# An indexer's products moved between projection products, its top-64 selection moved ahead, and a causal mask moved to another tile

## The chip, the cores and the metric

The kernel runs on one core of one Trainium2 chip. Its time is device time in microseconds (us) for one whole execution; the lower the better. The engines of a core work side by side, each through its own list of instructions: TensorE (PE in the profile; PEld is its weight load), VectorE (DVE), ScalarE (ACT), GpSimd (POOL) and SyncE (SP), which issues the DMA transfers. They wait for each other on counted semaphores.

## What is computed

The program is two transformer blocks on 256 tokens of width 1024, each with attention and a mixture of experts. The change lies in the mixer of the second block, after the first block's experts and before the recurrence of the second. All data is float32. One wide projection of the normed input gives, among others, queries (512 wide), a latent for keys and values (256), an indexer's query and key (8 heads of 32), and 15 groups of columns that are shifted by one token and mixed (called the shifted products here). The part that matters, for one block of 128 queries:

```python
dots = jnp.einsum('bthd,bsd->bths', qib, k_idx)
score = jnp.einsum('bths,bth->bts', jax.nn.relu(dots), wib) * idx_scale
score = jnp.where(causal[None], score, -jnp.inf)
_, sel = lax.top_k(score, top_k)          # top_k = 64 of 256
logits = jnp.einsum('bthd,btkhd->bthk', qb, k_sel) * (ATTN_HEAD_DIM ** -0.5)
logits = logits - slopes * dist           # dist = t - sel
logits = jnp.where(valid, logits, -jnp.inf)
p = jax.nn.softmax(logits, axis=-1)
# the shifted columns, for the recurrence that follows
mixed = p_shift + (prev - p_shift) * mu
# the modulation of the block
mod = jax.nn.silu(c) @ ada_w[i] + ada_b[i]
```

## The kernel before

Tokens lie in two halves (`t`) of 128. The code of a stage is split by engine: `project_*` and `sparse_*` follow each other in each engine's list, so their work overlaps. Order is by hand: each engine runs its list top to bottom and waits on semaphores.

**Projection and shifted products.** TensorE computes queries (`pj_q`), latent (`pj_kv`), indexer query (`pj_qi`), indexer key and head weights (`pj_ki`); ScalarE copies each out of PSUM (`pj_out`). A shifted product `m` of 0 to 14 (`shifted_product`, line 1806) accumulates 8 matmul pairs in the PSUM bank `SHIFT_BANKS[m]`. ScalarE evicts it with `shifted_own` (L1813), and VectorE adds the part of the previous token with `shifted_before` (L1820), which counts `mixed_done`. `SHIFT_NOW` of them come in `project_tensor`, those up to `LATE_SHIFT` = 11 in `sparse_tensor`, and the last four between head units. SyncE loads more gate weights when products 8, 12 and 15 are done.

**Modulation.** Rows of `ada_w_2` come in 8 chunks of 2 MB (`load_ada2`, L228) into two alternating slots of `side`. VectorE adds each with two instructions (`sum_ada2_rows`, L252, and `sum_ada2_cols`, L241); a chunk's load waits for the sums two chunks earlier.

**Indexer.** 16 dots (8 heads for each half, `dots`, L2077) each fill half a PSUM bank of banks 0 to 3; `relu` (L2185) evicts, `add_head` (L2237, L2239) weighs and sums into the tile `work`. It has four `rl` buffers. GpSimd masks each half (`affine_select`, L2061). VectorE then takes 8 rounds of `max` and `match_replace` (L2259, L2260) for each half, which leaves the 64 taken scores marked. `drop` turns the marks into 0 or -1, GpSimd masks it (L2065), and it is multiplied into the distance tile `dst2` (L2268).

**Attention.** The latent and the queries are transposed (L2087, L2092) and scaled by VectorE (`latT`, `qT2`); the up-projection makes keys and values (L2111); keys are normed (`head_norm`, L1839 to L1844, with a root on ScalarE) and transposed (L2119). Sixteen units (head and half) follow: `scores` (L2132), bias and mask by VectorE (`first`, L2276), `max`, exponential on ScalarE (L2209), a turn (L2142), the product with values (L2151).

**Later.** The recurrence, the merge of branches, and the second experts stage follow. SyncE issues the first expert load of that stage (`load_group`, L995) once VectorE has counted `or_done`.

Of the kernel before, what the change touches and what calls it, by code (L numbers as in the profile page):

```python
# [47 lines left out]
def build(nc, inp, out, debug=None, until=99):  # L48
    ctx = ExitStack()
    with ctx:  # L50
# [1699 lines left out]
        if debug and until <= 5:  # L1750
# [9 lines left out]
            "pj_out": ("pj_q_out", "pj_q_out", "pj_kv_out", "q_sq", "lat_sq", "lat_sq", "pj_qi_out", "pj_ki_out", "pj_ki_out", "lat_root", "q_root"),  # L1760
# [31 lines left out]
        SHIFT_NOW = 5  # L1792
        SHIFT_BANKS = [0, 1, 2, 3, 4, 7, 4, 7, 5, 6, 4, 7, 7, 7, 7]
# [28 lines left out]


# [37 lines left out]
        if True:  # L1861
# [55 lines left out]
            def project_tensor(pe):  # L1917
# [34 lines left out]
                for m in range(SHIFT_NOW):  # L1952
                    if m == 4:
                        pe.wait_ge(sem("pj_out"), at("pj_ki_out", 2))
                    shifted_product(pe, m)

            def project_scalar(act):
# [20 lines left out]
                act.wait_ge(sem("norm_vec"), at("lat_ms", 1))  # L1978
                act.activation(st6[:, 4:6], st6[:, 2:4], ACT.Sqrt).then_inc(sem("pj_out"), 1)
                act.wait_ge(sem("norm_vec"), at("q_ms", 1))  # L1980
                act.activation(st6[:, 32:48], st6[:, 16:32], ACT.Sqrt).then_inc(sem("pj_out"), 1)
# [37 lines left out]
        work = side[:, 4608:5120].rearrange("p (t s) -> p t s", t=NT)  # L2019
# [4 lines left out]
        rl = acc[:, 1024:2048].rearrange("p (b s) -> p b s", b=4)  # L2024
# [20 lines left out]
        if True:  # L2045
# [8 lines left out]
            def sparse_pool(pool):  # L2054
                pool.wait_ge(sem("ada2_rows_summed"), ADA2_CHUNKS)
                pool.wait_ge(sem("ada2_cols_summed"), ADA2_CHUNKS)
                pool.iota(dst2, pattern=[[P, NT], [-1, S]], base=0, channel_multiplier=1,
                          allow_small_or_imprecise_dtypes=True).then_inc(sem("dst2"), 1)
# [4 lines left out]
                pool.wait_ge(sem("drop_raw"), 1)  # L2063
                for t in range(NT):
                    pool.affine_select(out=drop[:, t, :], in_=drop[:, t, :], compare_op=ALU.is_ge, fill=-1.0, base=t * P,  # L2065
                                       pattern=[[-1, S]], channel_multiplier=1).then_inc(sem("drop"), 1)

            def sparse_tensor(pe):

                def dots(u):  # L2070
                    t, h = u // 8, u % 8
                    r = 32 * (h % 4)
                    if u >= 4:
                        pe.wait_ge(sem("idx_relu"), u - 3)
                    else:
                        pe.wait_ge(sem("mixed_done"), u + 1)
                    pe.matmul(ps[h % 4][:, 0:S], qiT[r:r + 32, h // 4, t * P:(t + 1) * P], kiT[r:r + 32, :],  # L2077
                              start=True, stop=True).then_inc(sem("idx_dots"), 1)
                for u in range(4):
                    dots(u)  # L2080
                shifted_product(pe, SHIFT_NOW)

                pe.wait_ge(sem("mixed_done"), SHIFT_NOW)
                pe.wait_ge(sem("norm_vec"), at("lat_normed", 1))
                for c in range(2):
                    for t in range(NT):
                        last = pe.transpose(ps[4][:, c * S + t * P:c * S + (t + 1) * P], kvl[:, t, c * P:(c + 1) * P], ident[:, :])  # L2087
# [978 lines left out]
```

## Time and profile before

| what | value |
|---|---|
| median of 3 runs | 1456.38 us (1456.31 to 1458.89) |
| the profiled execution | 1454.63 us |
| its span in the trace | 1452.9 us |
| mean granted TensorE clock (share of full) | 0.886 |
| TensorE busy | 1163.4 us, 80% |
| VectorE busy | 502.4 us, 35% |
| ScalarE busy | 265.6 us, 18% |
| GpSimd busy | 42.2 us, 3% |
| share of DMA in the chain that ended last | 25% |
| DMA moved | 404.66 MB, 279 GB/s mean |

All times inside the kernel are counted from the start of the span. A clock of 1.00 is 2.4 GHz and 0.50 is 1.2 GHz. In a timeline, a row merges instructions of one form that follow each other; the number in brackets is how long the engine stood idle before it, and who released it. A busy TensorE matmul row overlaps the next a little, because matmuls are pipelined.

### The profile page before, as it was taken

The numbers are of one execution on the slowest core, as the hardware profiler recorded it, in microseconds if no ns is written. First come the engines' busy times: TensorE is split into PE (matmuls) and PEld (weight loads), VectorE is DVE, ScalarE is ACT, GpSimd is POOL, SyncE is SP. The second block draws the span as 40 slices with busy tenths as digits, with TensorE's granted clock in tenths as the row PEclk, the third lists the DMA queues.
The fourth block names the chain that finished last, engine by engine and source line by source line (L and its number), as shares of the span: only waits on it lengthen the run. The fifth ranks groups of instructions, "written<-read, shape, count | busy, mean of one in ns | idle before, by whom it ended". The sixth has DMA issues, their size and how long they took to land. (4 is left out here: it accounts for less than half of the span.)

```text
span 1452.9 us, 16891 instructions
## 1 busy us (share of the span) xinstructions
PE 1163.4 (80%) x6663; PEld 677.1 (47%) x6663; DVE 502.4 (35%) x1285; ACT 265.6 (18%) x666; POOL 42.2 (3%) x109
## 2 busy tenths in 40 slices
PE   5999869999999693889999999979656567666666
PEld 2788444444343482566777776644121221221212
DVE  1569442222222526665644446342101011010111
ACT  2233212111121210234322220012010100101000
POOL 0000000000000200000101100000000000000000
PEclk8999879999999796898999997989877787778888
DMA  9877636999999748032001112555999999999995
GB/s 372 281 276 276 252 119 265 403 429 427 426 429 404 226 171 332 1 116 102 15 1 59 59 58 64 232 231 226 422 422 422 422 422 422 422 422 422 422 421 246
DMA packets 75149, 404.66 MB, mean 279 GB/s; under 512 B 14073, under 2 KB 15286, under 8 KB 41304
## 3 DMA queue, kind: packets, MB, share of 16 engines
q1 hardware_dynamic: 75096, 403.94, 68.9%
q8 instruction: 35, 0.57, 0.2%
q14 instruction: 18, 0.15, 0.0%
HBM read 402.88 MB, written 1.05 MB: 278 GB/s over the span
## 5 line engine op out<-in xcount | busy, mean ns | idle before, releaser
L1178 PE MATMUL ps<-ring,hT_sb 128*32 128x512 f32 x768 | 115.9, 759 | 72.8 <-DMA ring<-in_expert_w_gate 41.7
L1538 PE MATMUL ps<-ring,hT_sb 128*64 128x512 f32 x448 | 113.1, 594 | 3.5 <-ACT hT_sb L1609 1.8
L1178 PEld LDWEIGHTS ps<-ring,hT_sb 128*32 128x32 f32 x768 | 28.5, 135 | 154.5 <-issue 90.8
L1178 PE MATMUL ps<-side,hT_sb 128*32 128x512 f32 x256 | 42.9, 831 | 36.7 <-DMA side<-in_expert_w_up 18.9
L634 PE MATMUL ps<-hT_sb,ring 128*128 128x256 f32 x256 | 62.1, 393 | 2.7 <-ACT hT_sb L379 2.7
L1190 PE MATMUL ps<-ring,tmp 128*32 128x512 f32 x384 | 49.7, 664 | 18.2 <-DMA ring<-in_expert_w_down 18.2
L1244 ACT ACTIVATE hT_sb<-ps,modc 128x128 f32<-128x128 f32 x72 | 27.1, 457 | 191.3 <-PE ps L1161 191.3
L1806 PE MATMUL ps<-hT_sb,ring 128*128 128x256 f32 (+1 forms) x240 | 61.8, 419 | 0.0
L1538 PEld LDWEIGHTS ps<-ring,hT_sb 128*64 128x64 f32 x448 | 35.3, 137 | 55.0 <-issue 51.8
L1282 DVE TENSOR_TENSOR tmp<-ps,tmp 128x512 f32<-128x512 f32 x8 | 5.5, 692 | 151.8 <-ACT tmp L1252 151.8
L1546 PE MATMUL ps<-ring,tmp 128*64 128x512 f32 x256 | 56.7, 595 | 0.0
L634 PEld LDWEIGHTS ps<-hT_sb,ring 128*128 128x128 f32 x256 | 48.1, 195 | 13.7 <-issue 4.6
L1806 PEld LDWEIGHTS ps<-hT_sb,ring 128*128 128x128 f32 (+1 forms) x240 | 48.3, 205 | 10.7 <-issue 2.8
L1293 DVE COPY hT_sb<-ps 128x512 f32<-128x512 f32 x8 | 5.5, 692 | 134.8 <-PE ps L1190 134.8
L1609 ACT ACTIVATE hT_sb<-ps,modc 128x128 f32<-128x128 f32 x72 | 27.1, 457 | 127.0 <-PE ps L1528 127.0
L2628 PE MATMUL ps<-hT_sb,ring 128*128 128x128 f32 x384 | 49.2, 281 | 0.0
L2628 PEld LDWEIGHTS ps<-hT_sb,ring 128*128 128x128 f32 x384 | 44.7, 191 | 5.4 <-issue 4.5
L1178 PEld LDWEIGHTS ps<-side,hT_sb 128*32 128x32 f32 x256 | 9.8, 146 | 69.7 <-issue 26.5
L1190 PE MATMUL ps<-side,tmp 128*32 128x512 f32 x128 | 24.3, 931 | 19.8 <-DMA side<-in_expert_w_down 19.8
L1288 DVE TENSOR_TENSOR tmp<-ps,tmp 128x512 f32<-128x512 f32 x8 | 5.5, 692 | 92.2 <-PE ps L1178 92.2
L214 DVE SCALAR_TENSOR_TENSOR acc<-side,cond,acc 128x1024 f32<-128x1024 f32 x28 | 35.8, 1280 | 0.8
L1190 PEld LDWEIGHTS ps<-ring,tmp 128*32 128x32 f32 x384 | 12.1, 120 | 49.4 <-issue 26.7
(522 smaller groups left out, 1917.1 us busy)
## 6 DMA issues: line engine op xcount, KB each, us to landing
ring<-in_expert_w_gate SPq DMA_DIRECT2D x12, 4096.0 KB, 34.6
ring<-in_expert_w_up SPq DMA_DIRECT2D x12, 4096.0 KB, 34.7
ring<-in_expert_w_down SPq DMA_DIRECT2D x12, 4096.0 KB, 34.2
ring<-in_expert_w_down SPq DMA_DIRECT2D x16, 2048.0 KB, 15.5
ring<-in_expert_w_up SPq DMA_DIRECT2D x16, 2048.0 KB, 17.9
ring<-in_expert_w_gate SPq DMA_DIRECT2D x12, 2048.0 KB, 19.5
side<-in_ada_w SPq DMA_DIRECT2D x20, 1024.0 KB, 6.5
ring<-in_w_in SPq DMA_DIRECT2D x9, 2048.0 KB, 8.3
```

What stands on the lines that cost most here:

```text
L214: ins = v.scalar_tensor_tensor(a, w, s, a, ALU.mult, ALU.add)
L634: last = pe.matmul(ps[6][:, w * S:(w + 1) * S], cell(2 * w + h // 4)[:, c, (h % 4) * P:(h % 4 + 1) * P], hT[:, c, :], start=(c == 0), stop ...
L1178: last = pe.matmul(bank[es, :], xg[:, c, es], w[:, e, c % 4, :], start=(c == 0), stop=(c == KC - 1))
L1190: last = pe.matmul(out_ps[h][es, :], hidT[:, f, es], w[:, e, f % 2, h * 512:(h + 1) * 512], start=(f == 0), stop=(f == FC - 1))
L1244: last = act.activation(xg[:, c, :], (gate_ps, up_ps)[half][:, (c % 4) * P:(c % 4 + 1) * P], ACT.Identity, scale=modc[:, 2 * KC + c:2 * KC ...
L1282: v.tensor_tensor(hid, gate_ps[:, :], hid, ALU.mult).then_inc(sem("q_silu"), 1)
L1288: v.tensor_tensor(hid, up_ps[:, :], hid, ALU.mult).then_inc(sem("q_hid_done"), 1)
L1538: last = pe.matmul(bank[e * SLOTS:(e + 1) * SLOTS, :], xg[:, c, e * SLOTS:(e + 1) * SLOTS], dst(e, j, par)[:, c, :], start=(c == 0), stop= ...
L1546: last = pe.matmul(out_ps[h][e * SLOTS:(e + 1) * SLOTS, :], hidT[:, f, e * SLOTS:(e + 1) * SLOTS], dst(e, 2, 0)[:, f, h * 512:(h + 1) * 51 ...
L1609: last = act.activation(xg[:, c, :], (gate_ps, up_ps)[half][:, (c % 4) * P:(c % 4 + 1) * P], ACT.Identity, scale=modc[:, 2 * KC + c:2 * KC ...
L1806: last = pe.matmul(ps[SHIFT_BANKS[m]][0:n, 0:S], p2(i)[:, c, o:o + n], hT[:, c, :], start=(c == 0), stop=(c == KC - 1))
L2628: last = pe.matmul(gate_bank(i), p2(GATE0 + m // 4)[:, c, (m % 4) * P:(m % 4 + 1) * P], hT[:, c, t * P:(t + 1) * P], start=(c == 0), stop= ...
```

## The change

- In `project_tensor`, four dots stand ahead of each of the shifted products 0 to 3, and all 16 are done there; products 4 and 5 follow (`SHIFT_NOW` = 6). The wait for ScalarE's copies of indexer key and head weights comes ahead of all of them. Banks 0 to 3 are the dots' and banks 4 to 7 the shifted products'.
- ScalarE takes the two roots (latent and query norm) ahead of the indexer's copies; relus of four dots precede each `shifted_own`. `rl` has eight buffers.
- VectorE sums four chunks of the modulation, not two, ahead of the latent and query norms. After each of the chunks 4 to 7 it adds four heads and evicts one shifted product.
- Top-64 starts right behind. Turns of the latent, the queries and the keys, the key norm and the evictions 4 to 8 are put between its rounds (`BESIDE`); evictions 9 and 10 come behind the distance step.
- GpSimd makes the distance tile, masks both halves of the scores, and then writes 1.0e32 into the non-causal places of the distance tile. The two selects on `drop` are gone. `work` moves from `side` to `acc`.
- In `sparse_tensor` the order is: transposes of latent and queries, product 6, up-projection, product 7, key transposes, products 8 and 9, the first four scores, product 10. The square of the keys stands behind the second of ScalarE's four copies.

```diff
-            "pj_out": ("pj_q_out", "pj_q_out", "pj_kv_out", "q_sq", "lat_sq", "lat_sq", "pj_qi_out", "pj_ki_out", "pj_ki_out", "lat_root", "q_root"),
+            "pj_out": ("pj_q_out", "pj_q_out", "pj_kv_out", "q_sq", "lat_sq", "lat_sq", "lat_root", "q_root", "pj_qi_out", "pj_ki_out", "pj_ki_out"),
...
-        SHIFT_NOW = 5
-        SHIFT_BANKS = [0, 1, 2, 3, 4, 7, 4, 7, 5, 6, 4, 7, 7, 7, 7]
+        SHIFT_NOW = 6
+        SHIFT_BANKS = [4, 5, 6, 7, 4, 5, 6, 7, 4, 5, 6, 7, 7, 7, 7]
...
+        def dots(pe, u):
+            t, h = u // 8, u % 8
+            r = 32 * (h % 4)
+            if u >= 4:
+                pe.wait_ge(sem("idx_relu"), u - 3)
+            pe.matmul(ps[h % 4][:, 0:S], qiT[r:r + 32, h // 4, t * P:(t + 1) * P], kiT[r:r + 32, :],
+                      start=True, stop=True).then_inc(sem("idx_dots"), 1)
+
+        def relu(act, u):
+            act.wait_ge(sem("idx_dots"), u + 1)
+            if u >= RL:
+                act.wait_ge(sem("idx_added"), u - RL + 1)
+            act.activation(rl[:, u % RL, :], ps[u % 4][:, 0:S], ACT.Relu).then_inc(sem("idx_relu"), 1)
+
+        def add_head(v, u):
+            t, h = u // 8, u % 8
+            v.wait_ge(sem("idx_relu"), u + 1)
+            w = w_idx[:, t * 8 + h:t * 8 + h + 1]
+            if h == 0:
+                ins = v.tensor_scalar(work[:, t, :], rl[:, u % RL, :], w, None, ALU.mult)
+            else:
+                ins = v.scalar_tensor_tensor(work[:, t, :], rl[:, u % RL, :], w, work[:, t, :], ALU.mult, ALU.add)
+            ins.then_inc(sem("idx_added"), 1)
+            v.wait_ge(sem("idx_added"), u + 1)
+            if h == 7:
+                v.tensor_copy(st6[:, 200 + t:201 + t], work[:, t, 0:1]).then_inc(sem("idx_score"), 1)
...
-                for m in range(SHIFT_NOW):
-                    if m == 4:
-                        pe.wait_ge(sem("pj_out"), at("pj_ki_out", 2))
+                pe.wait_ge(sem("pj_out"), at("pj_ki_out", 2))
+                for m in range(4):
+                    for u in range(4 * m, 4 * m + 4):
+                        dots(pe, u)
+                    shifted_product(pe, m)
+                for m in range(4, SHIFT_NOW):
                     shifted_product(pe, m)
...
+                act.wait_ge(sem("norm_vec"), at("lat_ms", 1))
+                act.activation(st6[:, 4:6], st6[:, 2:4], ACT.Sqrt).then_inc(sem("pj_out"), 1)
+                act.wait_ge(sem("norm_vec"), at("q_ms", 1))
+                act.activation(st6[:, 32:48], st6[:, 16:32], ACT.Sqrt).then_inc(sem("pj_out"), 1)
...
-                for m in range(SHIFT_NOW):
+                for m in range(4):
+                    for u in range(4 * m, 4 * m + 4):
+                        relu(act, u)
+                    shifted_own(act, m)
+                for m in range(4, SHIFT_NOW):
                     shifted_own(act, m)
...
-                for k in range(2):
+                for k in range(4):
...
-                for k in range(2, ADA2_CHUNKS):
-                    if k >= 5:
-                        shifted_before(v, k - 5)
+                for k in range(4, ADA2_CHUNKS):
                     sum_ada2_rows(v, k)
                     sum_ada2_cols(v, k)
-                for m in range(3, SHIFT_NOW):
-                    shifted_before(v, m)
+                    for u in range(4 * (k - 4), 4 * (k - 4) + 4):
+                        add_head(v, u)
+                    shifted_before(v, k - 4)
...
-        work = side[:, 4608:5120].rearrange("p (t s) -> p t s", t=NT)
+        work = acc[:, 5120:5632].rearrange("p (t s) -> p t s", t=NT)
...
-                pool.iota(dst2, pattern=[[P, NT], [-1, S]], base=0, channel_multiplier=1,
-                          allow_small_or_imprecise_dtypes=True).then_inc(sem("dst2"), 1)
+                p_step(pool.iota(dst2, pattern=[[P, NT], [-1, S]], base=0, channel_multiplier=1,
+                                 allow_small_or_imprecise_dtypes=True))
                 for t in range(NT):
                     pool.wait_ge(sem("idx_score"), t + 1)
                     pool.affine_select(out=work[:, t, :], in_=work[:, t, :], compare_op=ALU.is_ge, fill=-BIG, base=t * P,
                                        pattern=[[-1, S]], channel_multiplier=1).then_inc(sem("idx_causal"), 1)
-                pool.wait_ge(sem("drop_raw"), 1)
                 for t in range(NT):
-                    pool.affine_select(out=drop[:, t, :], in_=drop[:, t, :], compare_op=ALU.is_ge, fill=-1.0, base=t * P,
-                                       pattern=[[-1, S]], channel_multiplier=1).then_inc(sem("drop"), 1)
+                    ins = pool.affine_select(out=dst2[:, t, :], in_=dst2[:, t, :], compare_op=ALU.is_ge, fill=1.0e32, base=t * P,
+                                             pattern=[[-1, S]], channel_multiplier=1)
+                ins.then_inc(sem("dst2"), 1)
...
+                pe.wait_ge(sem("idx_relu"), 16)
                 pe.wait_ge(sem("norm_vec"), at("lat_normed", 1))
...
+                shifted_product(pe, SHIFT_NOW)
...
+                shifted_product(pe, SHIFT_NOW + 1)
                 pe.wait_ge(sem("norm_vec"), at("k_normed", 1))
+                pe.wait_ge(sem("turn_out"), at("qT_done", 4))
...
-                for u in range(4):
-                    scores(u)
-
-                pe.wait_ge(sem("kv_out"), 4)
-                for m in range(SHIFT_NOW + 1, LATE_SHIFT):
+                for m in range(SHIFT_NOW + 2, LATE_SHIFT):
+                    if m == LATE_SHIFT - 1:
+                        for u in range(4):
+                            scores(u)
                     shifted_product(pe, m)
                 pe.wait_ge(sem("mixed_done"), LATE_SHIFT)
...
+                    if i == 1:
+                        act.wait_ge(sem("kv_out"), 2)
+                        act.activation(sq6, side[:, 0:1024], ACT.Square).then_inc(sem("k_act"), 1)
...
+                BESIDE = {1: (4,), 3: (5,), 4: (turn_lat, turn_q), 5: (6,), 6: ("k", 7), 7: (turn_k, 8)}
...
-                    if r in (3, 4, 6, 7):
-                        shifted_before(v, {3: 6, 4: 7, 6: 8, 7: 9}[r])
-                shifted_before(v, 10)
-                v.tensor_scalar(drop, work, TAKEN, 1.0, ALU.is_equal, ALU.subtract).then_inc(sem("drop_raw"), 1)
+                    for x in BESIDE.get(r, ()):
+                        if x == "k":
+                            head_norm(v, sq6, 48, "k_act", "k", side[:, 0:1024])
+                        elif isinstance(x, int):
+                            shifted_before(v, x)
+                        else:
+                            x()
+                v_step(v.tensor_scalar(drop, work, TAKEN, 1.0, ALU.is_equal, ALU.subtract))
                 v.wait_ge(sem("dst2"), 1)
-                v.wait_ge(sem("drop"), 2)
-
                 v_step(v.scalar_tensor_tensor(dst2, drop, -1.0e32, dst2, ALU.mult, ALU.add))
+                for m in range(9, LATE_SHIFT):
+                    shifted_before(v, m)
```

## Rows read from the trace of the kernel before

**Rows 1.** The chain that ended last, in order of time (start us, us, what).

```profile
979.63 0.07 issue
...
1010.37 29.20 DMA side<-in_expert_w_gate
```

**Rows 2.** Timeline of SyncE's queue (start us, us, engine, line, operation), 680 to 1010.

```profile
909.91 17.57 SPq L995 DMA_DIRECT2D ring<-in_expert_w_gate  x2
```

**Rows 3.** Stretches: length, each engine's busy us (instructions), TensorE's granted clock, DMA share, GB/s.

```profile
520.00:525.00 5.00, 5.00 (x25) 4.41 (x24) 0.17 (x1) 2.33 (x6) 0.00 (x0) 1.00 0.68 251
535.00:540.00 5.00, 5.00 (x17) 4.10 (x16) 4.63 (x6) 0.65 (x2) 0.00 (x0) 0.66 0.00 2
585.00:600.00 15.00, 11.73 (x53) 6.25 (x51) 9.52 (x21) 7.53 (x19) 0.40 (x1) 1.00 0.00 1
631.00:638.00 7.00, 6.53 (x22) 4.87 (x23) 3.81 (x14) 2.71 (x10) 0.00 (x0) 0.52 0.01 2
674.00:910.00 236.00, 218.22 (x1764) 179.12 (x1762) 127.87 (x365) 62.48 (x177) 22.31 (x53) 0.94 0.14 48
```

**Rows 4.** Timeline of VectorE, 510 to 690 (idle before it and its releaser in brackets).

```profile
534.82 0.17 DVE L2002 RECIPROCAL acc<-acc 128x2 f32<-128x2 f32 x1 [11.88 <-ACT acc L1979]
...
550.85 2.35 DVE L252 SCALAR_TENSOR_TENSOR gate_rows<-side,cond,gate_rows 128x2048 f32<-128x2048 f32 x1 [2.96 <-DMA side<-in_ada_w]
...
561.16 2.35 DVE L252 SCALAR_TENSOR_TENSOR gate_rows<-side,cond,gate_rows 128x2048 f32<-128x2048 f32 x1 [5.30 <-DMA side<-in_ada_w]
...
578.20 0.87 DVE L1820 SCALAR_TENSOR_TENSOR ring<-ps,colsB,ring 128x255 f32<-128x255 f32 x2
...
588.92 3.61 DVE L2239 SCALAR_TENSOR_TENSOR side<-acc,small,side 128x256 f32<-128x256 f32 x7
...
596.78 1.22 DVE L1839 TENSOR_REDUCE acc<-acc 128x16 f32<-128x1024 f32 x1 [4.05 <-ACT acc L2197]
...
605.59 0.41 DVE L2259 MAX8 acc<-side 128x8 f32<-128x256 f32 x1
...
607.54 0.43 DVE L2259 MAX8 acc<-side 128x8 f32<-128x256 f32 x1
...
629.68 0.42 DVE L2276 SCALAR_TENSOR_TENSOR acc<-side,ps 128x256 f32<-128x256 f32 x1
```

**Rows 5.** Timeline of SyncE's queue, 500 to 680.

```profile
543.39 0.33 SPq L228 DMA_DIRECT2D side<-in_ada_w  x1
...
547.92 18.21 SPq L228 DMA_DIRECT2D side<-in_ada_w  x3
```

**Rows 6.** Timeline of TensorE, 500 to 680.

```profile
530.57 3.63 PE L1945 MATMUL ps<-tmp,hT_sb 128*128 128x8 f32 x32
534.06 19.20 PE L1806 MATMUL ps<-hT_sb,ring 128*128 128x256 f32 x80
...
579.88 5.30 PE L1806 MATMUL ps<-hT_sb,ring 128*128 128x256 f32 x16
...
585.45 1.04 PE L2092 MATMUL ps<-ident,tmp 128*128 128x128 f32 x8
586.42 1.11 PE L2077 MATMUL ps<-tmp 32*128 32x256 f32 x8
587.46 3.70 PE L2111 MATMUL ps<-ring,side 128*128 128x512 f32 x8
...
607.73 18.85 PE L1806 MATMUL ps<-hT_sb,ring 128*128 128x256 f32 x80
...
643.03 0.70 PE L2132 MATMUL ps<-side 64*128 64x256 f32 x4
```

**Rows 7.** Timeline of ScalarE, 500 to 680.

```profile
527.32 0.60 ACT L1973 ACTIVATE tmp<-ps 128x512 f32<-128x512 f32 x1 [4.57 <-PE ps L1937]
...
627.11 1.28 ACT L2209 ACT_TABLE_LOAD   x1
```

**Rows 8.** Timeline of GpSimd, 500 to 680.

```profile
604.25 0.40 POOL L2061 TENSOR_SCALAR_AFFINE_SELECT side<-side 128x256 f32<-128x256 f32 x1 [10.97 <-DVE acc L2243]
```

More of the change, by code:

```diff
@@ L2086, in sparse_tensor @@
                     for t in range(NT):
-                        last = pe.transpose(ps[4][:, c * S + t * P:c * S + (t + 1) * P], kvl[:, t, c * P:(c + 1) * P], ident[:, :])
+                        last = pe.transpose(ps[2][:, c * S + t * P:c * S + (t + 1) * P], kvl[:, t, c * P:(c + 1) * P], ident[:, :])
                 last.then_inc(sem("turn_psum"), 1)
@@ L2091, in sparse_tensor @@
                     for t in range(NT):
-                        last = pe.transpose(ps[5 + c // 2][:, (c % 2) * S + t * P:(c % 2) * S + (t + 1) * P],
+                        last = pe.transpose(ps[c // 2][:, (c % 2) * S + t * P:(c % 2) * S + (t + 1) * P],
                                             q_tok[:, t, c * P:(c + 1) * P], ident[:, :])
                 last.then_inc(sem("turn_psum"), 1)
-                for u in range(4, 8):
-                    dots(u)
+                shifted_product(pe, SHIFT_NOW)
                 pe.wait_ge(sem("kv_up_loaded"), 16)
-                pe.wait_ge(sem("mixed_done"), SHIFT_NOW + 1)
                 pe.wait_ge(sem("turn_out"), at("latT_done", 2))
@@ L2102, in sparse_tensor @@
                     for t in range(NT):
-                        if n == 0 and t == 1:
-                            pe.wait_ge(sem("turn_out"), at("latT_done", 2))
                         if n == 1:
                             pe.wait_ge(sem("kv_out"), t + 1)
-                            if t == 0:
-                                pe.wait_ge(sem("turn_out"), at("qT_done", 4))
-                        b = ps[7] if (t == 0) else ps[4]
                         for c in range(2):
-                            last = pe.matmul(b[:, :], latT[:, c, t * P:(t + 1) * P], kv_up[:, c, n * 512:(n + 1) * 512],
+                            last = pe.matmul(ps[3 - t][:, :], latT[:, c, t * P:(t + 1) * P], kv_up[:, c, n * 512:(n + 1) * 512],
                                              start=(c == 0), stop=(c == 1))
                         last.then_inc(sem("kv_psum"), 1)
-                for u in range(8, 16):
-                    dots(u)
+                shifted_product(pe, SHIFT_NOW + 1)
                 pe.wait_ge(sem("norm_vec"), at("k_normed", 1))
+                pe.wait_ge(sem("turn_out"), at("qT_done", 4))
                 for c in range(4):
                     for t in range(NT):
-                        last = pe.transpose(ps[5 + c // 2][:, (c % 2) * S + t * P:(c % 2) * S + (t + 1) * P],
+                        last = pe.transpose(ps[c // 2][:, (c % 2) * S + t * P:(c % 2) * S + (t + 1) * P],
                                             k_tok[:, t, c * P:(c + 1) * P], ident[:, :])
@@ L2179, in sparse_scalar @@
             def sparse_scalar(act):
-                def relu(u):
-                    act.wait_ge(sem("idx_dots"), u + 1)
-                    if u >= 4:
-                        act.wait_ge(sem("idx_added"), u - 3)
-                    act.activation(rl[:, u % 4, :], ps[u % 4][:, 0:S], ACT.Relu).then_inc(sem("idx_relu"), 1)
                 shifted_own(act, SHIFT_NOW)
-                for u in range(8):
-                    relu(u)
                 act.wait_ge(sem("ada2_rows_summed"), ADA2_CHUNKS)
@@ L2244, in sparse_vector, with turn_lat @@
-                for u in range(8):
-                    add_head(u)
-                head_norm(v, sq6, 48, "k_act", "k", side[:, 0:1024])
-                for u in range(8, 16):
-                    add_head(u)
-                v.wait_ge(sem("turn_psum"), at("k_psum", 1))
-                for c in range(4):
-                    v.tensor_scalar(kT2[:, c, :], ps[5 + c // 2][:, (c % 2) * S:(c % 2 + 1) * S], colsB[:, nB + 1:nB + 2], None,
-                                    ALU.mult).then_inc(sem("turn_out"), 1)
+                def turn_lat():
+                    v.wait_ge(sem("turn_psum"), at("lat_psum", 1))
+                    for c in range(2):
+                        v.tensor_scalar(latT[:, c, :], ps[2][:, c * S:(c + 1) * S], colB("kv_norm_g_2", c), None, ALU.mult).then_inc(
+                            sem("turn_out"), 1)
@@ new lines, in turn_q, with turn_k @@
+                def turn_q():
+                    v.wait_ge(sem("turn_psum"), at("q_psum", 1))
+                    for c in range(4):
+                        v.tensor_scalar(qT2[:, c, :], ps[c // 2][:, (c % 2) * S:(c % 2 + 1) * S], qk_cols[:, 1:2], None,
+                                        ALU.mult).then_inc(sem("turn_out"), 1)
+                def turn_k():
+                    v.wait_ge(sem("turn_psum"), at("k_psum", 1))
+                    for c in range(4):
+                        v.tensor_scalar(kT2[:, c, :], ps[c // 2][:, (c % 2) * S:(c % 2 + 1) * S], colsB[:, nB + 1:nB + 2], None,
+                                        ALU.mult).then_inc(sem("turn_out"), 1)
```

50 lines of the change are left out of this document (4 added, 46 removed).

## The prediction

> **What bounds the kernel now.** I read the page first: its chain of work that ended last is mostly transfers of expert weights. Followed in order of time, the chain begins only at 979.6 us, and from 1010 us on nearly every long piece of it is such a transfer [rows 1]. So the end is a stream of fixed length. What can be won is an earlier start of it, and the chain says nothing of the stage that the change edits. The SyncE queue says when the stream starts: its first expert load goes out at 909.91, behind a wait on the branch results (`or_done`) that VectorE makes [rows 2]. Between 674 and 910 TensorE is 92% busy and the DMA moves 48 GB/s [rows 3]: that stretch is compute, ordered by waits among engines, and each load in it is issued on a signal of an engine, not at a fixed time. A shift of the attention stage should therefore reach the end one for one.
>
> In the attention stage I read the VectorE timeline, then TensorE's. VectorE waits until 534.82 for a root that ScalarE runs behind its copies, then waits for three of the modulation's weight chunks (2.96 us for chunk 4, 5.30 for chunk 5), since a chunk's load needs the sum two chunks back [rows 4, 5]. TensorE finishes its five shifted products at about 553.3 and then does next to nothing till 579.9: each indexer product waits for an evicted bank, and the evictions stand between the sums [rows 6]. Only at 605.59 does top-64 start. The first biased logits come at 629.68 [rows 4]. That instruction is my mark: what it gains, the kernel gains.
>
> **The change, laid out in time.** I place the new order on the trace's clock; until about 500 us nothing differs.
>
> *Loads and sums.* Now four chunks are summed before the latent norm. The DMA has delivered all that was issued by about 523 (it moved 251 GB/s from 520 to 525 and its next load is issued at 543.39), chunk 3 ahead of the last weights [rows 3, 5]. One chunk costs VectorE two instructions of 2.35 us, 2.27 from start to start, so 4.54 us [rows 4]. Sums 2 and 3 fit from about 513 to 522.5, where VectorE idled, and cost nothing; if they had no such gap they would cost 9.1 us. Chunk 4 can then be asked for at about 517 instead of 543.39 and chunk 5 at 522.6 instead of 547.9 [rows 5]. SyncE is freed earlier for the weights queued behind them, p2_load(4) and p2_load(5). The two roots moved ahead of the indexer's copies should end at about 526; ScalarE idled 4.57 us before the first of those copies at 527.32, so they delay none [rows 7].
>
> *Dots, products, evictions.* TensorE now waits for both copies and starts at 534.8 instead of 534.06, +0.7 us (the root behind these copies released VectorE at 534.82) [rows 4, 6]. Four dots take 1.11 us at the full clock [rows 6]; one shifted product takes 3.45 (five take 18.85 with a slow start, and 3.45 is what separates their evictions). The first five took 19.20, so product 0 took about 5.4: the granted clock was 0.66 of full from 535 to 540 though TensorE was busy [rows 3, 6]. I keep that loss of 1.9 us, part of it (0.3) now on dots: dots end 536.1, product 0 at 540.9, its two evictions at 542.05 (0.2 + 0.47 ScalarE, then 0.40 VectorE). Chunk 4's sum ends near 532.5 and heads 0 to 3 are added before 539, so VectorE waits for this eviction before sum 5, and everything later in the stretch hangs on it.
>
> From 542.05, three rounds of sum (4.54), four head sums (4 x 0.516 = 2.06, from seven in 3.61) and one eviction (0.40; two take 0.87, overlapping a little) are 7.0 us each [rows 4]. Chunk 6 was asked for at 532.6. Chunk 7 is asked for at 546.6 and needed at 556.1, 9.5 us later; the load issued at 543.39 took 7.5 us till its sum began [rows 4, 5]. The last head sum ends at 542.05 + 21.0 - 0.4 = 562.65. GpSimd masks in 0.40, plus 0.3 for two hand-overs [rows 8]: top-64 starts at 563.35, against 605.59. TensorE has four groups of 4.56, two products and the transposes of latent and queries (about 1.4) and product 6; it is done at 566.2. Its waits on relu have slack: relu 15 needs head 7 added, which is so at 548.7.
>
> *Work moved into the rounds.* A round of top-64 for both halves is 1.95 us [rows 4]. Five rounds and evictions 4 and 5 (0.8) end at 573.9, and the two turns of the latent, each as large as an eviction (0.87 for both), bring 574.75. Here lies the new stall: the latent up-projection, queued on TensorE ahead of product 7, waits for it from 566.2, and with it ScalarE's key copies and the key norm. From there TensorE sets the mark: up-projection 2 x 3.45 (its 3.70 overlaps the next), product 7 3.45, key transposes 1.0 (the query's eight took 1.04), products 8 and 9 6.9, four scores 1.35 (two take 0.70), product 10 3.45 [rows 6]. That is 23.05. To it comes the clock: after waits like this one TensorE ran at 1.2 GHz, and the product at 579.88 took 5.30, a loss of 1.85 [rows 6]. Lower bound 0 (the clock holds), upper 3.5 (6.9 us at half the clock do the work of 3.45); I take 2.4, between this 1.85 and the loss of about 3 behind the first unit's wait, where the clock stood at 0.52 from 631 to 638 [rows 3]. 574.75 + 23.05 + 2.4 = 600.2. Two evictions (0.2 + 0.47 + 0.40): VectorE's first biased logits at 601.3.
>
> *VectorE beside it.* Rounds 5 to 7, the key norm (3.1 us, 596.78 to the next head sum), the key's and query's turns and evictions 6 to 9 amount to some 15 us in the 26.5 between 574.75 and 601.3, so they are hidden, although the wait for product 7 holds round 7 back to about 588.5. If VectorE had no slack there, the worst is the key norm plus a turn, 4.7 us. The mask in the distance tile takes GpSimd's two selects out of the path. Before, they and the drop and distance steps stood between the last eviction and the logits (the eviction that needs product 10, whose five end at 626.6, and the mark at 629.68 [rows 4, 6]: 3.1 us). Now drop and distance run at about 593 to 594, under product 9, and 1.1 us remain between product 10 and the mark. These 2 us are in the difference of the marks already. The exponential's table load (1.28, at 627.11 right behind the last eviction by ScalarE) now runs from 600.9 to 602.15; the first maximum is ready at 602.3, 1.0 behind the mark, so the load stays hidden by 0.15 us; at worst it costs 0.3 [rows 7].
>
> **Sum.** Mark 629.68 - 601.3 = 28.4 us. The 16 head units behind the mark keep their order and banks. Profiled execution 1454.63 (span 1452.9) gives 1426.2. The median shown is 1456.38, 1.75 above it, so I predict 1456.4 - 28.4 = **1428.0 us**.
>
> **Rivals.**
> 1. *The chunks stay late (0.10).* Chunk 5 took 13.2 us before, sharing the DMA with other weights [rows 4, 5]. If chunk 7 takes that too it lands at 559.9, not 556.1: +3.7, 1431.7. For it: weights p2(5) follow in the queue. Against it: they follow chunk 7 in the queue and do not precede it.
> 2. *More low clock or a stall among the rounds (0.07).* Product 0 wholly slow (+1.5) and the key norm uncovered (+4.7) give about 1434. ScalarE and TensorE slack above speaks against it.
> 3. *The clock stays up (0.07).* The wait before the up-projection costs nothing (-2.4) and the wait behind product 10, 2.9 instead of 4.9 us, no longer slows the 6 us of work behind it (-3.1) [rows 3, 6]: 1422.5.
> 4. *The gain is given back at a later wait (0.02).* A load of the recurrence or of the experts would have to be bound to an absolute time: 1456.4. The queue shows none.
> 5. *Slower (0.03): interleaved narrow dots hold TensorE at 1.2 GHz.* All of its 53 us of work from 534.8 to 600.2 then take twice as long: 4 x 9.1, then 13.8, 2.8, 6.9 put the up-projection at 594.7 and product 10 at 640.7, the mark at 641.8: +12.1, 1468.5. It decides once some 41 of the 53 us run at the low clock (28.4 of gain, 8.6 of TensorE's own wait, and the 4.3 that I assume already). For it: the clock was low at 535 to 540 right after the 8-column products. Against it: from 585 to 600 dots, transposes and copies alternated and the clock was 1.00 [rows 3, 6]. The Trainium skill, page "TensorE: Matmul & The Clock Gate", section "A second HAM failure mode: psum-queue depth-cycling", says that small idle gaps between groups of matmuls that cycle through PSUM banks can make the clock swing between its two levels. By that page rival 5 would gain weight; this trace's 585 to 600 does not show it.
>
> **How the numbers follow.** The forecast holds 0.71, with its own range 1424.5 to 1431.5. Rivals 1 to 3 lie inside 1422 to 1436, which is my range; outside it are rivals 4 and 5 and a tail. "No change" means within 0.2%, 2.9 us, about what a measurement of this kernel can tell from nothing. Faster 0.95, same 0.02, slower 0.03.
>
> **What the profile after will show.** Top-64 starts near 563, the up-projection near 575 after a wait of some 8 us, the first biased logits near 601; the first expert load is issued near 881.5. Dots come in four groups with products between and no waits on evictions. The clock is 1.00 between about 541 and 569. I am wrong if chunk sums wait for DMA after 550, if TensorE is at half clock across the dots, or if the first expert load moves by less than the mark.

## The result and the profile after

The changed kernel takes 1419.34 us (median of 4 runs, 1417.30 to 1421.82) against 1456.35 us (4 runs, 1455.33 to 1458.89): ratio 0.9744, 95% interval 0.9723 to 0.9765, so 37 us less. I had forecast 28.4 us less and a range that ended at 1422. The direction was right, and the sum fell short by 8.7 us. The profiled execution took 1417.3 us, 37.3 less than the one of before.

The page of the changed kernel, its span and the granted clock in 40 slices:

```profile
span 1415.6 us, 16890 instructions
...
PEclk8999878999999799899999997979778787888888
```

SyncE's queue and the chain that ended last, of the changed kernel (start us, us, what):

```profile
873.23 17.25 SPq L995 DMA_DIRECT2D ring<-in_expert_w_gate  x2
```

```profile
942.64 0.07 issue
```

The first expert load goes out 36.7 us earlier than in [rows 2], and the chain begins 37.0 earlier than in [rows 1]. From that load to the end of the span it is 543.0 us before and 542.4 after, so nearly all that was won was won before it. (Over all 14 profiles of this document this last part took 542.2 to 545.2 us; it is fixed only to some 3 us.) VectorE's timeline of the changed kernel, in answer to [rows 4]:

```profile
519.81 2.35 DVE L252 SCALAR_TENSOR_TENSOR gate_rows<-side,cond,gate_rows 128x2048 f32<-128x2048 f32 x1 [0.29 <-DMA side<-in_ada_w]
...
530.07 2.35 DVE L252 SCALAR_TENSOR_TENSOR gate_rows<-side,cond,gate_rows 128x2048 f32<-128x2048 f32 x1 [1.27 <-DMA side<-in_ada_w]
...
541.63 0.48 DVE L1820 SCALAR_TENSOR_TENSOR ring<-ps,colsB,ring 128x255 f32<-128x255 f32 x1 [3.49 <-ACT ring L1813]
...
555.96 2.34 DVE L252 SCALAR_TENSOR_TENSOR gate_rows<-side,cond,gate_rows 128x2048 f32<-128x2048 f32 x1
...
563.28 0.43 DVE L2250 MAX8 acc<-acc 128x8 f32<-128x256 f32 x1
...
573.89 0.88 DVE L2229 TENSOR_SCALAR side<-ps,colsB 128x256 f32<-128x256 f32 x2
...
596.35 0.48 DVE L1820 SCALAR_TENSOR_TENSOR ring<-ps,colsB,ring 128x255 f32<-128x255 f32 x1 [1.98 <-ACT ring L1813]
601.00 0.48 DVE L1820 SCALAR_TENSOR_TENSOR ring<-ps,colsB,ring 128x255 f32<-128x255 f32 x1 [4.16 <-ACT ring L1813]
601.39 0.41 DVE L2271 SCALAR_TENSOR_TENSOR acc<-side,ps 128x256 f32<-128x256 f32 x1
```

And TensorE's, in answer to [rows 6]:

```profile
535.01 0.77 PE L1829 MATMUL ps<-tmp 32*128 32x256 f32 x8 [0.64 <-ACT small L2011]
535.71 5.30 PE L1806 MATMUL ps<-hT_sb,ring 128*128 128x256 f32 x16
...
561.95 3.62 PE L1806 MATMUL ps<-hT_sb,ring 128*128 128x256 f32 x16
574.92 9.58 PE L2125 MATMUL ps<-ring,side 128*128 128x512 f32 x16 [9.35 <-DVE side L2229]
...
596.73 3.72 PE L1806 MATMUL ps<-hT_sb,ring 128*128 128x256 f32 x16
603.18 0.41 PE L2156 MATMUL ps<-ident,acc 128*128 128x128 f32 x2 [2.73 <-issue]
```

The reader is to see two things. Up to the mark (the first biased logits, L2276 before and L2271 after) the layout holds almost to the tenth: top-64 at 563.28 (forecast 563.35), the start of the up-projection at 574.92 (574.75), 9.42 us from there to the start of product 7 (9.3), the mark at 601.39 (601.3). The wait ahead of the up-projection was 9.35 us, where the forecast gives 8.55. The mark came 28.3 us earlier. Behind it, where the code is the same in both, another 8.4 us went: from the mark to the first expert load it is 280.2 us before and 271.8 after.

Where they went shows in a table of stretches, cut at the same distances behind the mark (10.3, 20, 11, 12 us). Columns as in [rows 3]; the number ahead of the DMA share is the granted clock. The kernel before:

```profile
629.70:640.00 10.30, 8.53 (x33) 6.71 (x34) 6.27 (x22) 3.33 (x11) 0.19 (x2) 0.67 0.01 2
640.00:660.00 20.00, 18.44 (x113) 13.79 (x112) 12.20 (x47) 10.03 (x33) 0.00 (x0) 1.00 0.31 105
660.00:671.00 11.00, 8.86 (x44) 5.25 (x43) 4.28 (x17) 2.77 (x9) 0.00 (x0) 0.84 0.16 40
671.00:683.00 12.00, 12.00 (x39) 9.43 (x39) 9.52 (x18) 5.31 (x11) 0.00 (x0) 0.57 0.36 139
```

The changed kernel:

```profile
601.40:611.70 10.30, 8.52 (x42) 6.50 (x42) 6.40 (x23) 5.08 (x15) 0.00 (x0) 0.83 0.01 2
611.70:631.70 20.00, 17.66 (x109) 13.44 (x107) 13.31 (x51) 9.53 (x32) 0.00 (x0) 1.00 0.31 106
631.70:642.70 11.00, 9.64 (x57) 6.84 (x58) 4.95 (x19) 4.67 (x12) 0.00 (x0) 1.00 0.44 148
642.70:654.70 12.00, 12.00 (x78) 10.20 (x77) 11.79 (x14) 10.35 (x18) 0.00 (x0) 1.00 0.57 195
```

The units and the preparation of the recurrence run at 1.2 GHz for about 6.8, 3.5 and 10.3 us before (twice the missing clock share times the length: (1 - 0.67) x 10.3 x 2, and so on), and for 3.5 us in all after. That difference of 17 us at half the clock is worth at most 8.5 us, and the two timelines drift apart by 1.4 us at the second unit, by 3.0 at the last, and by 7.4 at the reciprocal of the preparation (687.78 before, 652.11 after). The last 1.0 us goes with one more low stretch, which runs up to the first expert load in both kernels. It begins 19.6 us ahead of that load before and 16.8 us ahead of it after (an estimate from the clock shares of the last 20 us, before first):

```profile
889.91:909.91 20.00, 19.32 (x176) 13.16 (x176) 12.14 (x26) 2.85 (x7) 1.12 (x5) 0.51 0.25 76
853.23:873.23 20.00, 18.39 (x176) 12.25 (x176) 12.53 (x27) 2.85 (x7) 1.12 (x5) 0.58 0.27 83
```

The question for the experiments was what made the clock differ.

### The profile page after: what moved, and what is told of

Same layout as the page of the kernel before. It is cut to its first block and busy times, and to the rows that moved or that the text cites. A ratio compares the mean times of both kernels' runs of the same rounds, so it can differ in the third digit from the quotient of the medians.

```text
span 1415.6 us, 16890 instructions
## 1 busy us (share of the span) xinstructions
PE 1145.7 (81%) x6663; PEld 665.5 (47%) x6663; DVE 502.5 (35%) x1285; ACT 265.5 (19%) x666; POOL 42.1 (3%) x109
## 5 line engine op out<-in xcount | busy, mean ns | idle before, releaser
L1178 PEld LDWEIGHTS ps<-ring,hT_sb 128*32 128x32 f32 x768 | 28.4, 134 | 154.8 <-issue 90.7
L1806 PE MATMUL ps<-hT_sb,ring 128*128 128x256 f32 (+1 forms) x240 | 57.7, 394 | 0.0
L634 PEld LDWEIGHTS ps<-hT_sb,ring 128*128 128x128 f32 x256 | 48.2, 195 | 13.8 <-issue 4.6
L1806 PEld LDWEIGHTS ps<-hT_sb,ring 128*128 128x128 f32 (+1 forms) x240 | 44.9, 192 | 9.3 <-issue 2.2
L2623 PE MATMUL ps<-hT_sb,ring 128*128 128x128 f32 x384 | 49.2, 281 | 0.0
```

Of the source, the lines that this page charges most:

```text
L634: last = pe.matmul(ps[6][:, w * S:(w + 1) * S], cell(2 * w + h // 4)[:, c, (h % 4) * P:(h % 4 + 1) * P], hT[:, c, :], start=(c == 0), stop ...
L1178: last = pe.matmul(bank[es, :], xg[:, c, es], w[:, e, c % 4, :], start=(c == 0), stop=(c == KC - 1))
L1806: last = pe.matmul(ps[SHIFT_BANKS[m]][0:n, 0:S], p2(i)[:, c, o:o + n], hT[:, c, :], start=(c == 0), stop=(c == KC - 1))
L2623: last = pe.matmul(gate_bank(i), p2(GATE0 + m // 4)[:, c, (m % 4) * P:(m % 4 + 1) * P], hT[:, c, t * P:(t + 1) * P], start=(c == 0), stop= ...
```

## The experiments

Two theories. The first: the instants at which the clock can fall or rise are not tied to the work, so which waits cost something is decided by where they happen to lie, and a small shift moves the end by something other than itself. The rival: the new order keeps TensorE's waits short (2.73 us instead of 4.9 ahead of the first unit), so the 8.4 us belong to the change. Profiles of different runs of one order place top-64 up to 2.5 us apart, so I compare the mark with an earlier instruction of the same trace, or give the time behind the mark ("tail": from the mark to the first expert load). The groups of runs were measured on different chips, each with the kernel before beside it (medians 1454.31 to 1457.03), so ends of different groups are compared by their ratios.

**Delays.** VectorE fills a tile that is not in use, ahead of the turn of the latent (changed kernel) or of the keys (before). One fill took 0.91 us, and from one to the next it is 1.19.

```diff
                 def turn_lat():
+                    for _ in range(2):        # or 4
+                        v_step(v.memset(side[:, 6144:7168], 0.0))
```

> The changed kernel, with two dummy fills of an unused 128x1024 tile (about 0.6 us each) on VectorE ahead of the latent's turn: everything behind it starts about 1.3 us later, nothing else differs. Where the instants at which TensorE's clock falls and rises are not tied to the work (first theory), the first biased logits come 1.3 us later but the end moves by something else, between 0 and +9 us, because other waits of the head units and of the preparation now meet a fall. Where the new order of the work is what keeps the clock up (rival), the end moves by 1.3 us and the clock falls once between 601 and 670, as in the changed kernel.

> As the run with two fills, with four: 2.6 us later. First theory: the end moves by something between 0 and +10 us, and not twice what two fills gave. Rival: +2.6 us.

> The kernel before, with two such fills on VectorE ahead of the turn of the keys, which TensorE's first scores and VectorE's top-64 both wait for: everything behind starts about 1.3 us later. First theory: the end moves by anything between +1.3 and -7 us, since the three low stretches behind the first biased logits (6.8, 3.4 and 10.2 us) need not recur. Rival: +1.3 us, with the three low stretches.

> As the run before, with four fills: 2.6 us later. The first biased logits then stand to the clock's instants about as in the changed kernel, so the first theory expects the low stretches behind them to shrink from 20 us towards 3 and the end to come earlier although work was added: some -5 us. Rival: +2.6 us.

Measured, with the profile's numbers beside the medians:

| kernel | median us | ratio to before (95%) | mark | tail |
|---|---|---|---|---|
| before | 1456.35 | | 629.68 | 280.2 |
| changed | 1419.34 | 0.9744 (0.9723 to 0.9765) | 601.39 | 271.8 |
| after_late2 | 1422.74 | 0.9784 (0.9750 to 0.9819) | 603.63 | 272.1 |
| after_late4 | 1433.68 | 0.9839 (0.9821 to 0.9857) | 607.34 | 281.0 |
| before_late2 | 1460.36 | 1.0020 (1.0009 to 1.0031) | 634.02 | 280.4 |
| before_late4 | 1454.30 | 0.9984 (0.9974 to 0.9994) | 634.55 | 274.5 |

Four fills cost the changed kernel 14.3 us (13.8 by the ratios), although they keep VectorE busy for only 3.6: counted from top-64 the mark comes 4.1 us later (607.34 - 565.15 against 601.39 - 563.28), and the tail is 9.1 us longer. Two fills cost 3.4 and left the tail alone. On the kernel before, two fills cost 3.3 us and left the tail alone too, while four made the end come earlier (1454.30 against 1457.03 for the kernel before beside it, interval below 1): 3.6 us of useless VectorE work more, 2.7 us less time. The stretches of the changed kernel with four fills, cut like those above:

```profile
607.30:617.60 10.30, 8.48 (x32) 6.57 (x33) 6.07 (x22) 4.23 (x12) 0.00 (x0) 0.67 0.01 2
...
637.60:648.60 11.00, 8.96 (x42) 5.10 (x42) 4.46 (x18) 2.72 (x9) 0.00 (x0) 0.84 0.12 30
648.60:660.60 12.00, 11.91 (x38) 9.33 (x39) 9.50 (x19) 5.47 (x11) 0.00 (x0) 0.57 0.39 148
```

They are the low stretches of the kernel before, clock for clock, in the order of the changed one. The rival, by which four fills move the end by about their own length and leave the tail alone, falls. So does its reason, the shorter wait ahead of the first unit: that wait is 2.73 us in the changed kernel and in after_late4 alike, with 3.4 us of low clock behind it in the one and 6.8 in the other. My sizes were loose: a fill took 0.91 us, not 0.6, and before_late4 shrank its low stretches from 20 to 10 us, not to 3.

**One part alone, and one part undone.** The mask on the kernel before, and the old mask on the changed kernel:

```diff
-                pool.wait_ge(sem("drop_raw"), 1)
                 for t in range(NT):
-                    pool.affine_select(out=drop[:, t, :], in_=drop[:, t, :], compare_op=ALU.is_ge, fill=-1.0, base=t * P,
-                                       pattern=[[-1, S]], channel_multiplier=1).then_inc(sem("drop"), 1)
+                    ins = pool.affine_select(out=dst2[:, t, :], in_=dst2[:, t, :], compare_op=ALU.is_ge, fill=1.0e32, base=t * P,
+                                             pattern=[[-1, S]], channel_multiplier=1)
...
-                v.wait_ge(sem("drop"), 2)
```

> The kernel before with one part of the change alone: GpSimd writes the causal mask into the distance tile ahead of time instead of into the drop tile in the path. It takes out VectorE's wait for GpSimd (1.01 us before), so the first biased logits come 1.0 us earlier. If a shift were carried through one for one, the end would come 1.0 us earlier; by the theory of the clock's instants it moves by that plus something between -7 and +4 us from the low stretches behind.

> The changed kernel with the old mask (GpSimd's two selects on the drop tile in the path). In the new order drop and distance run under product 9, where VectorE then waits 1.98 us for ScalarE's eviction, so the wait for GpSimd (about 1.0) is hidden: first biased logits unmoved, end within 0.5 us of the changed kernel. Rival: the mask carries part of the gain here too, and the mark comes 1 us later.

before_mask: 1446.15 us, ratio 0.9937 (0.9916 to 0.9957). From top-64 to the mark it took 23.2 us instead of 24.1, so the mark gained 0.9, as expected. The end gained about 9, more than I had allowed, since the tail fell from 280.2 to 271.9. TensorE's wait ahead of the first unit is 3.92 us instead of 4.89, and only 3.4 us of low clock followed:

```profile
631.64 0.41 PE L2142 MATMUL ps<-ident,acc 128*128 128x128 f32 x2 [3.92 <-issue]
...
634.26 2.59 PE L1806 MATMUL ps<-hT_sb,ring 128*128 128x256 f32 x8
```

The half product that took 2.59 us here took 3.57 in the kernel before and 1.95 at the full clock.

after_old_mask: 1419.44 us, ratio 0.9751 (0.9733 to 0.9769), 0.1 us from the changed kernel; top-64 to mark 38.1 us in both. Its VectorE timeline shows the cover that I had named:

```profile
596.22 0.69 DVE L2263 SCALAR_TENSOR_TENSOR side<-side 128x512 f32<-128x512 f32 x1 [1.01 <-POOL side L2099]
597.91 0.48 DVE L1820 SCALAR_TENSOR_TENSOR ring<-ps,colsB,ring 128x255 f32<-128x255 f32 x1 [0.99 <-ACT ring L1813]
```

The wait for GpSimd is back (1.01), and the wait for the eviction behind it is shorter by as much (0.99 instead of 1.98). In the new order the mask carries nothing.

**The chunks.**

```diff
-                for k in range(4):            # ahead of the latent norm
+                for k in range(2):
...
+                for k in (2, 3):              # behind the query norm
+                    sum_ada2_rows(v, k)
+                    sum_ada2_cols(v, k)
```

> The changed kernel, but only two chunks of the modulation are summed ahead of the latent and query norms; chunks 2 and 3 come behind them. Their 9.1 us are no longer in VectorE's gap, and the loads of chunks 4 to 7 are asked for 8 to 13 us later, so VectorE waits for the DMA again. I expect top-64 to start at about 571 instead of 563.3 and the first biased logits 8 us later. If this part carried nothing, both would stay.

1435.18 us, ratio 0.9862 (0.9843 to 0.9881): 15.8 us slower than the changed kernel (17 by the ratios). Top-64 starts at 572.3, 9.0 us later where I had put 8, and the mark is at 609.4, 8.0 us later, as expected; the waits for the DMA are back:

```profile
539.65 2.35 DVE L252 SCALAR_TENSOR_TENSOR gate_rows<-side,cond,gate_rows 128x2048 f32<-128x2048 f32 x1 [2.92 <-DMA side<-in_ada_w]
551.06 2.35 DVE L252 SCALAR_TENSOR_TENSOR gate_rows<-side,cond,gate_rows 128x2048 f32<-128x2048 f32 x1 [4.45 <-DMA side<-in_ada_w]
```

The tail is the long one, 280.3 us, so the rest is again clock.

**TensorE kept at work.** The direct test of what the low clock costs: matmuls whose result nobody reads, in the wait ahead of the first unit (10 on the kernel before, 5 on the changed one, with and without the four fills).

```diff
+                pe.wait_ge(sem("mixed_done"), 8)
+                for _ in range(10):
+                    pe.matmul(ps[7][:, S:2 * S], ident[:, :], hT[:, 0, :], start=True, stop=True)
                 pe.wait_ge(sem("mixed_done"), LATE_SHIFT)
```

> The kernel before with ten matmuls whose result nobody reads (128x256, about 0.43 us each at the full clock), placed on TensorE in its 4.9 us wait ahead of the first head unit. They move nothing ahead of the first biased logits. If the low clock behind that wait is what makes the stretch from the mark to the first expert load 280.2 us long instead of 271.8, the first low stretch (6.8 us from 630.9) goes and the end comes 2 to 8 us earlier, although work was added. If the low clock costs nothing because other engines set the pace of the units, the end stays within 1 us.

> The changed kernel with five such matmuls in its 2.7 us wait ahead of the first unit. There only 3.4 us of low clock are behind the mark, so at most 1.7 us are to be had: end 0 to 2 us earlier than the changed kernel.

> The changed kernel delayed by four dummy fills (3.6 us of VectorE time ahead of the latent's turn, which alone cost 14.3 us at the end, 8 to 9 of them behind the mark), and with the five matmuls ahead of the first unit. If the wait ahead of the first unit is where the loss behind the mark begins, the filler brings the tail back from 281.0 to about 272 and the end to about 1424. If the loss comes from where the later waits happen to lie, the tail stays at 278 or more and the end near 1432.

| kernel | median us | ratio to before (95%) | mark | tail |
|---|---|---|---|---|
| before_filled | 1447.18 | 0.9947 (0.9932 to 0.9962) | 631.31 | 270.7 |
| after_filled | 1417.38 | 0.9746 (0.9732 to 0.9760) | 601.90 | 271.8 |
| after_filled_late4 | 1425.13 | 0.9802 (0.9785 to 0.9820) | 606.85 | 272.5 |

Added work alone made the kernel before 7.1 us faster (1454.31 to 1447.18, measured side by side). The stretches of before_filled behind its mark:

```profile
631.30:641.60 10.30, 9.28 (x56) 7.04 (x54) 7.32 (x26) 5.43 (x18) 0.23 (x2) 1.00 0.12 30
...
661.60:672.60 11.00, 9.76 (x57) 6.94 (x56) 5.22 (x17) 5.16 (x12) 0.00 (x0) 1.00 0.55 192
672.60:684.60 12.00, 12.00 (x86) 10.66 (x85) 11.83 (x11) 10.32 (x16) 0.00 (x0) 1.00 0.51 175
```

All three low stretches are gone, the later two as well, though nothing was put into the waits ahead of those. Its tail, 270.7 us, is 9.5 shorter than that of before and about that of the changed kernel, and nothing of the change is in it. On the changed kernel the filler brings nothing that can be told from zero (ratio 0.9746 against 0.9744), and the tail stays at 271.8. The low stretch behind the first unit's wait is gone there, but another of the same length appears 29.8 us behind the mark, where the changed kernel has none:

```profile
601.90:612.20 10.30, 9.28 (x56) 7.04 (x54) 7.33 (x27) 6.30 (x19) 0.00 (x0) 1.00 0.13 30
...
632.20:643.20 11.00, 9.76 (x51) 6.49 (x50) 3.66 (x14) 3.54 (x8) 0.00 (x0) 0.87 0.42 149
```

With four fills the filler takes 8.5 us off the tail (281.0 to 272.5), again with one low stretch of 3.4 us among the units, 28.9 us behind the mark. The end comes 8.6 us earlier by the medians and 5.4 by the ratios (0.9839 to 0.9802), of the 13.8 that the fills had cost.

**A better order among the rounds.** The new stall of 9.35 us ahead of the up-projection can go:

```diff
-                BESIDE = {1: (4,), 3: (5,), 4: (turn_lat, turn_q), 5: (6,), 6: ("k", 7), 7: (turn_k, 8)}
+                BESIDE = {0: (turn_q,), 1: (4,), 2: (5, 6, "k"), 3: (turn_k,), 4: (7,), 5: (8,), 6: (9,)}
+                turn_lat()
...
-                for m in range(9, LATE_SHIFT):
+                for m in range(10, LATE_SHIFT):
                     shifted_before(v, m)
```

> The changed kernel with the work among the rounds in another order: VectorE turns the latent ahead of round 0 instead of behind round 4, the queries behind round 0, evictions 4, 5, 6 and the key norm behind rounds 1 and 2, the key turn behind round 3, evictions 7, 8, 9 behind rounds 4, 5, 6. The up-projection then follows product 6 with no wait (9.35 us in the changed kernel) and at the full clock. From the trace after: product 6 ends 565.4, then 6.9 + 3.45 + 1.0 + 3.45 + 3.45 + 1.1 + 3.45, first biased logits at about 589.7 instead of 601.4: -11.7 us. VectorE's own work (26.6 us from 563.3) ends at about the same time. The end moves by -11.7, plus or minus up to 5 from the low clock behind. Rival: VectorE becomes the bound, because the key norm waits for ScalarE and the rounds queue behind it: mark at 593 to 595.

> The version with the latent turned ahead of round 0, with six such matmuls ahead of the first unit. Its mark came 9.4 us earlier than in the changed kernel (11.7 expected), its tail was 279.0 instead of 271.8. If the filler takes the low stretches off the tail, the end comes to about 1406 to 1408; if not, it stays at 1413.

latent_first: 1413.61 us (1409.32 to 1417.99), ratio 0.9704 (0.9671 to 0.9737). TensorE no longer waits:

```profile
563.92 3.62 PE L1806 MATMUL ps<-hT_sb,ring 128*128 128x256 f32 x16
567.38 7.03 PE L2125 MATMUL ps<-ring,side 128*128 128x512 f32 x16
```

From the last chunk's sum (557.92) to the mark (591.98) it takes 34.1 us instead of 45.4 (555.96 to 601.39), 11.4 less where I had put 11.7. The end gained only 5.7, since the tail grew to 279.0: the clock again. With six filler matmuls: 1410.44 us (1409.50 to 1413.01), ratio 0.9701 (0.9686 to 0.9716), tail 275.7, with one low stretch of 10.2 us left in the preparation. The profiled tail is 3.3 us shorter, but the two ratios cannot be told apart, so what the filler gives at the end is not shown here. These two are the fastest versions measured, some 6 us below the changed kernel by the ratios, and the filled one is 2 to 4 us above what I had expected of it.

**All profiles together.** Two readings over all 14 traces say more than any pair. First, the tail follows the time that the granted clock of the trace stands at 1.2 GHz between the mark and the first expert load: with 20 to 22 us of it (seven traces) the tail is 270.7 to 272.5 us, with 28.0 it is 274.5, with 29.8 it is 275.7, with 36.5 it is 279.0, and with 40 us (four traces) 280.2 to 281.0. That is about 0.44 us of tail for each microsecond at the low clock, in both orders, delayed or not, filled or not. Second, the first theory's "not tied to the work" is too strong. In every trace a long low stretch begins 49.2 to 50.0 us ahead of the 8-column products (530.57 in [rows 6]), so from one execution to the next the clock fell at the same place of the work within 0.8 us. That fits lengths that recur from run to run, and a delay that shifts what stands behind it against the falls. A difference below 1 us is enough for another outcome: of the five traces of the old order, which have the same code up to there, two have the low stretch of 535.3 to 538.7 and three do not (7 us of the kernel before, then of before_late2):

```profile
534.00:541.00 7.00, 7.00 (x26) 5.88 (x26) 5.79 (x7) 1.24 (x5) 0.00 (x0) 0.76 0.00 1
534.00:541.00 7.00, 7.00 (x39) 6.30 (x40) 4.78 (x7) 1.24 (x5) 0.00 (x0) 1.00 0.01 4
```

## Why the prediction was right and where it was wrong

- *Chunks, DMA, roots:* right. Sums 2 and 3 fit VectorE's gap, VectorE waited 0.29 and 1.27 us for chunks 3 and 4 without effect, and not at all behind 550. Undone, this part costs 8 us at the mark. Rival 1 did not occur.
- *Dots and product 0:* right at the point that sets the pace, the low clock of 535 to 540 included (0.66 again); eviction 0 at 541.63, to end at 542.05 by forecast and at 542.1 in the trace. Four dots took 0.65 us from their start to that of the product behind them and not the 1.11 of the forecast, so TensorE was done at 565.4 instead of 566.2 and only waited longer. That narrow dots hold the clock down (rival 5) did not show: product 0 and what follows ran as laid out, and the granted clock from 541 to 569 was 1.00. The Trainium skill, page "TensorE: Matmul & The Clock Gate", section "A second HAM failure mode: psum-queue depth-cycling", describes a clock that swings because TensorE idles briefly between groups of matmuls. Here it did not swing, but TensorE was busy for all of the 24 us from 541 to 565, so the stretch had none of those idle gaps and does not test the page.
- *The up-projection as the new stall:* right in place (9.35 us of wait) and price (2.4 us of low clock forecast; 9.42 from its start to product 7's instead of 6.9 is 2.5). The wait itself was 0.8 us longer than laid out, for the dots' sake.
- *Mask:* right that it is hidden in the new order (0.1 us undone). The exponential's table load stayed hidden by 0.2 us.
- *The step that failed:* "The 16 head units behind the mark keep their order and banks", and with it "A shift of the attention stage should therefore reach the end one for one". Order and banks did stay, but not the clock they are run at. I took the tail as a constant of 280 us. It is 271 to 281, depending on how much of it runs at the low clock. So the sum held the mark (28.4 forecast, 28.3 measured) and put at nothing a term behind it that measured 8.4 us. Rival 3 had the mechanism at the right wait, but I gave it 3.1 us, for the 6 us of low clock right behind that wait, and a chance of 0.07. At that wait the low clock became shorter (6.8 to 3.5 us) but did not go, and by the second unit 1.4 us were won. The rest of the 8.4 comes from the later low stretches (3.5 and 10.3 us), which the changed kernel does not have, and from the shorter one ahead of the expert load; the forecast named none of them. Its other half, no loss ahead of the up-projection, did not happen.

So of 37.3 us of the profiled difference, 28.3 are the new order up to the mark, 8.4 the clock behind it, 0.6 the expert stage. The 8.4 are not bound to the new order: the filler alone gives 9.5 of tail to the kernel before, and four fills take 9.1 from the changed one. That the changed kernel got them is luck: no part of its order was made for them. Shown is that moving a wait by a few microseconds, or filling it, switches these stretches. Not shown is what decides over the second and third. In the two kernels compared they came and went with the first, but they don't always: before_late4 has the first and second without the third, after_filled the second alone, and latent_first_filled the third alone. A filler in front of each of them alone wasn't tried, nor was the tail mapped for shifts between those measured.

## What to carry to other kernels

In this kernel a stage of short dependent steps had more than one length with the same code (271 to 281 us), because TensorE's clock fell around some of its waits and not around others. When such a stage is moved, give it both lengths in the forecast, and read them from the low stretches of the trace of before (their length, and half of it as the loss) rather than shift the stage as a block. To tell a gain of order from one of clock, delay the stage by two and by four microseconds, or put unread matmuls into the wait ahead of it, and then look in the trace whether a low stretch has only moved (after_filled); here the clock alone was worth up to 9 us (0.6%), so a gain of that size that stands on neither should not be put down to the order.

## What the runs showed of the hardware that was not expected

- Useless work in the path made a kernel faster: four fills of 0.91 us on VectorE, 1457.03 to 1454.30 us. So did ten unread matmuls in a wait of TensorE, 1454.31 to 1447.18 us.
- Taking 1.0 us of wait out of the path (before_mask), which made one TensorE wait 3.92 us instead of 4.89, took 8.4 us off the 280 us behind it. Whether the shorter wait or the shift did it is not separated.
- The length is steady from run to run in some versions: 19 runs of the kernel before on one chip lie within 1454.15 and 1459.41 us, and the four of after_late4 within 1431.73 and 1434.58. In others it isn't: ten runs of the kernel before on another chip span 1451.07 to 1461.34, seven of before_mask 1443.76 to 1451.48, four of latent_first 1409.32 to 1417.99, and after_late2 had one run of four at 1430.58, the others at 1420.96 to 1423.64. Only one execution of each has a trace, so which low stretches the slower ones had is not known.
